# First block of a two-block transformer kernel: the 31-tap convolution as Toeplitz products on TensorE, rotary tiles of four heads, attention in pairs of heads

## What is computed

```
proj = rms_norm(h, g_mix_pre) @ w_in       # w_in 1024 x 1696: q_a 384 | kv_a 256 | k_rope 32 | conv 2 x 512
q  = rms_norm(q_a) @ w_q_b                 # 8 heads of 64 plain + 32 rotary columns
kv = rms_norm(kv_a) @ w_kv_b               # 8 heads of 64 key + 64 value columns
q_rope, k_rope = apply_rope(...)           # x1*cos - x2*sin, x1*sin + x2*cos
attn = causal softmax((q_nope.k_nope + q_rope.k_rope) * 96**-0.5) @ v
a, gate = split(conv)
c = causal_depthwise_conv(a * sigmoid(gate), conv_w, conv_b)   # 31 taps, 512 channels
c = silu(layer_norm(c, conv_ln_g, conv_ln_b))
mix = concat([attn, c]) @ w_o              # w_o 1024 x 1024
h = h + rms_norm(mix, g_mix_post)
```

## Time and profile before

| | us |
|---|---|
| median of 3 runs | 2088.38 |
| the profiled execution's own time | 2087.02 |
| its span (first to last instruction) | 2085.2 |
| TensorE busy | 1899.2 (91%) |
| VectorE busy | 1111.9 (53%) |
| ScalarE busy | 712.1 (34%) |
| GpSimd busy | 776.4 (37%) |
| mean granted TensorE clock | 0.944 |

### The profile page before, as it was taken

One profiled execution on the slowest core, in us unless ns is written; L12 is line 12 of the kernel. 1 busy time (PEld: TensorE's weight loads), 2 busy tenths in 40 slices (PEclk: granted clock), 3 DMA queues, 4 the chain that ended last, 5 costly groups with the idle time before them and its releaser, 6 DMA issues.

```text
span 2085.2 us, 24117 instructions
## 1 busy us (share of the span) xinstructions
PE 1899.2 (91%) x8716; PEld 1523.6 (73%) x8716; DVE 1111.9 (53%) x1734; ACT 712.1 (34%) x1162; POOL 776.4 (37%) x323
## 2 busy tenths in 40 slices
PE   7957775899999979999999999999978899999997
PEld 5735453788888757788888888898755578888885
DVE  6987837844344566333634443740488727333444
ACT  4234333322222234213322222332368833222221
POOL 3344031353444333434544454344300034444541
PEclk9977887999999989999999999997879999999998
DMA  5211011133233222495332323233111122333331
GB/s 174 67 54 41 11 61 41 61 104 98 85 112 95 85 72 85 91 195 139 122 93 88 101 92 110 81 101 101 46 26 31 52 64 86 106 98 91 91 94 57
DMA packets 52170, 177.34 MB, mean 85 GB/s; under 512 B 5528, under 2 KB 5912, under 8 KB 52089
## 3 DMA queue, kind: packets, MB, share of 16 engines
q1 hardware_dynamic: 47952, 166.22, 25.4%
q10 hardware_dynamic: 4136, 10.02, 3.4%
HBM read 166.75 MB, written 9.47 MB: 85 GB/s over the span
## 4 chain that ended last, share of the span: by engine, by line
PE 78%; DVE 16%; ACT 3%; issue 2%; DMA 0%; POOL 0%; DVEq 0%; ACTq 0%
PE ps L394 25%; PE ps L395 24%; PE ps L396 24%; DVE arena L1333 4%; DVE acc L1261 1%; DVE arena L1905 1%; DVE arena L1888 1%; PE ps L749 1%; PE ps L726 1%; DVE h L1517 1%; PE ps L714 1%; DVE rstd L1266 1%; DVE arena L1515 1%; DVE arena L1448 1%; PE ps L448 1%
## 5 line engine op out<-in xcount | busy, mean ns | idle before, releaser
L351 POOL TENSOR_TENSOR WL<-raw,WH 128x1024 fp32r<-128x1024 f32 x301 | 751.0, 2510 | 1257.9 <-ACT WH L788 1257.9
L394 PE MATMUL ps<-XH,WH 128*128 128x512 f32 (+1 forms) x1296 | 512.4, 395 | 61.4 <-DVE XL L1271 32.8
L395 PE MATMUL ps<-XL,WH 128*128 128x512 f32 (+1 forms) x1296 | 508.5, 392 | 0.0
L396 PE MATMUL ps<-XH,WL 128*128 128x512 f32 (+1 forms) x1296 | 508.0, 392 | 0.0
L788 ACT ACTIVATE WH<-raw 128x1024 fp32r<-128x1024 f32 x301 | 309.9, 1052 | 545.5 <-PE ps L396 492.7
L394 PE MATMUL ps<-HH,WH 128*128 128x512 f32 x1056 | 419.6, 397 | 35.7 <-DVE arena L1415 18.0
L396 PE MATMUL ps<-HH,WL 128*128 128x512 f32 x1056 | 415.5, 393 | 0.0
L395 PE MATMUL ps<-HL,WH 128*128 128x512 f32 x1056 | 415.5, 393 | 0.0
L394 PEld LDWEIGHTS ps<-XH,WH 128*128 128x128 f32 x1296 | 252.0, 194 | 121.9 <-issue 47.7
L396 PEld LDWEIGHTS ps<-XH,WL 128*128 128x128 f32 x1296 | 252.1, 195 | 49.5
L395 PEld LDWEIGHTS ps<-XL,WH 128*128 128x128 f32 x1296 | 252.2, 195 | 48.8 <-issue 0.7
(11 more groups left out here) (207 smaller groups left out, 1675.0 us busy)
## 6 DMA issues: line engine op xcount, KB each, us to landing
raw<-in_weights SPq DMA_DIRECT2D x301, 512.0 KB, 3.6
tab<-arena ACTq DMA_DIRECT2D x1, 5120.0 KB, 78.4
arena<-tab SPq DMA_DIRECT2D x16, 256.0 KB, 3.7
ftab<-arena ACTq DMA_DIRECT2D x1, 2080.0 KB, 23.7
h<-in_xT SPq DMA_DIRECT2D x8, 256.0 KB, 7.9
out_T<-h SPq DMA_DIRECT2D x8, 256.0 KB, 2.1
arena<-ftab ACTq DMA_DIRECT2D x4, 256.0 KB
arena<-in_pT ACTq DMA_DIRECT2D x1, 512.0 KB, 3.6
```

What stands on the lines that cost most here:

```text
L351: nc.gpsimd.tensor_tensor(WL[:, s, :], raw[:, s, :], WH[:, s, :].bitcast(f32), SUB)\
L394: nc.tensor.matmul(out, wh, xh, start=start, stop=False)
L395: nc.tensor.matmul(out, wh, xl, start=False, stop=False)
L396: return nc.tensor.matmul(out, wl, xh, start=False, stop=stop)
```

## The change

On TensorE: each of the 8 groups of 64 channels becomes 16 float32 matmuls of 128 rows, 128 outputs and 256 columns (`conv_group`). `U` holds even tokens of a group in partitions 0 to 63 and odd tokens in 64 to 127, with 15 columns of zeros ahead; `tz` holds, for one group, the diagonal blocks of the tap values. VectorE makes `tz` by one multiplication of 2048 elements a row (`lag_products`), two buffers deep, and ScalarE takes the results out of PSUM with the bias (`conv_out`). `CPE = 4` puts all four channel tiles there, so `convolve` has no steps left. In w_in the conv units come first (`SOURCE`), then q_a, k_rope, kv_a.

The rotary table fills 128 partitions, and the columns of w_q_b and of k_rope are regrouped while ScalarE and GpSimd split the weights (`pieces`, 3 instructions instead of one for each of two units of w_in, 6 for each pair of w_q_b units). Four heads' rotary rows come out of one tile. Attention runs in 4 pairs, as in the second block, with 32-row matmuls added for the rotary part; the maximum is no longer found and scaled in steps of its own. The layer norm of the convolution is spread over the attention loop, its sums over channels are made by four float32 matmuls each (`ln_total`), and w_o starts with the conv rows, between the transposes and products of the last pairs.

The diff, cut to its core:

```diff
+CPE = 4
+GPE, LAGS = 2 * CPE, 16
+        WOH = [XH[:, 6, :], XH[:, 7, :], HH[:, 2, :], HH[:, 3, :]] + [XH[:, c, :] for c in range(4)]
+        SOURCE = [0, 1, 2, 3, 8, 9, 12, 13, 4, 5, 6, 7, 10, 11] + list(range(14, 20)) + [...]
+        KEYS1, HEADS1 = (10, 11), (14, 16)
...
+            def conv_group(g):
+                if g >= 4:
+                    pe.wait_ge(sems["ce_done"], 2 * (g - 3))
+                pe.wait_ge(sems["tz_ok"], g + 1)
+                pe.wait_ge(*m["u_ok"].next(2))
+                for k in range(LAGS):
+                    at = 64 * (2 * LAGS - 2 - 2 * k)
+                    last = nc.tensor.matmul(ps[:, 4 + g % 4, 256 * (g // 4):256 * (g // 4) + 256], tz[:, g % 2, at:at + P],
+                                            U[:, g, LAGS - 1 - k:UW - k], start=k == 0, stop=k == LAGS - 1,
+                                            skip_group_check=True)
+                last.then_inc(sems["tz_used"], 1)
+            def ln_total(x, ready, done):
+                for c in range(4):
+                    ready(c)
+                    last = nc.tensor.matmul(ps[:, 6, :], ones[:, :], x[:, c, :], start=c == 0, stop=c == 3)
+                last.then_inc(sems[done], 1)
+            def mla_scores(n, step):
...
+                for qs in STEPS2[step]:
+                    w, at, q = P * (qs + 1), P * (qs == 1), slice(qs * P, (qs + 1) * P)
+                    for k, (low, of) in enumerate(((XH, HH), (XH, HL), (XL, HH))):
+                        for r in range(2):
+                            nc.tensor.matmul(ps[:, 2 * (c % 2) + r, at:at + w], low[HALF[r], n, q],
+                                             of[HALF[r], KN[n], 0:w], start=k == 0, stop=False)
+                    for k, (low, of) in enumerate(((XH, HH), (XH, HL), (XL, HH))):
+                        for r in range(2):
+                            i = 32 * (2 * (n % 2) + r)
+                            last = nc.tensor.matmul(ps[:, 2 * (c % 2) + r, at:at + w], low[i:i + 32, 4 + n // 2, q],
+                                                    of[i:i + 32, KRR, 0:w], start=False, stop=k == 2)
...
             project(2, 4, 2, XH, XL, m["x_lo"])
             total(7)
-            for _ in range(4):
+            for _ in range(6):
                 project(2, 4, 2, XH, XL)
             total(2)
-            for _ in range(2):
-                project(2, 4, 2, XH, XL)
+            conv_group(0)
             total(1)
+            for g in range(1, GPE):
+                if g == 3:
+                    pe.wait_ge(sems["norm_std"], m["norm_sum"].n)
+                conv_group(g)
...
+            ln_total(cacc, convolved, "ln_sum")
+            for n in range(NP1 + 2):
+                if n < NP1:
+                    if n % 2 == 0:
+                        pe.wait_ge(sems["q1_lo"], n // 2 + 1)
+                    mla_scores(n, 0)
+                    mla_scores(n, 1)
+                if n >= 2:
+                    mla_values(n - 2)
+                if n == 1:
+                    ln_total(lnsq, lambda c: pe.wait_ge(sems["ln_sq"], c + 1), "ln_var")
+                if n < NP1:
+                    mla_scores(n, 2)
+                if n == NP1:
+                    pe.wait_ge(sems["l1_done"], 8 * NP1)
+                    w_o((0, 1), m["cv_lo"])
+                if 1 <= n <= NP1:
+                    for r in range(2):
+                        mla_transposes(n - 1, r)
+                if n == NP1:
+                    w_o((1, 2), m["cv_lo"])
-            project(4, 2, 4, XH, XL, m["x_lo"], part=(0, 2))
-            total(3)
-            pe.wait_ge(*m["conv_xc"].next(4))
-            total(3)
-            project(4, 2, 4, XH, XL, m["x_lo"], part=(2, 4))
-            project(4, 2, 4, XH, XL)
+            w_o((2, 4), m["at_lo"])
+            project(4, 2, 4, WOH, WOL, cols=lambda x, c: x[c])
             total(7)
...
+            def conv_out(g):
+                act.wait_ge(sems["tz_used"], g + 1)
+                ch = 8 - GPE + g
+                for f in range(2):
+                    nc.scalar.activation(cacc[64 * (ch % 2):64 * (ch % 2) + 64, ch // 2, 1 - f::2],
+                                         ps[HALF[f], 4 + g % 4, 256 * (g // 4):256 * (g // 4) + 256], ACT.Identity,
+                                         bias=small[HALF[f], BIAS2 + g:BIAS2 + g + 1])\
+                      .then_inc(sems["ce_done"], 1)
...
+            def lag_products(g):
+                if g >= 2:
+                    dve.wait_ge(sems["tz_used"], g - 1)
+                V.tensor_tensor(tz[:, g % 2, :].rearrange("p (e n) -> p e n", n=64),
+                                stack.unsqueeze(1).to_broadcast([P, 2 * LAGS, 64]),
+                                taps_of[:, g, :].unsqueeze(2).to_broadcast([P, 2 * LAGS, 64]), MUL).then_inc(sems["tz_ok"], 1)
...
-            for n in range(H1 + 1):
-                if n < H1:
-                    logits(n, JOBS1[n])
-                if n >= 1:
-                    normalise(n - 1, JOBS1[n - 1])
-                convolve(8)
```

More of the change, by code:

```diff
@@ L481, in values @@
                 for g, kts in enumerate(VALUES):
-                    pe.wait_ge(*m["pt_act"].upto(3 * n + g + 1))
+                    if g == 0:
+                        pe.wait_ge(sems["p1_g0"], 2 * n + 2)
+                    else:
+                        pe.wait_ge(sems["p1_rest"], 4 * n + 2 + g)
                     for kt, at in kts:
-                        done = nc.tensor.matmul(job.out[:, kt * P:S], job.v(kt), job.pt(n)[:, at:at + S - kt * P],
-                                                start=first and kt == 0, stop=last and (g, kt) == (2, 2),
-                                                skip_group_check=True)
@@ L487, in values @@
-                done.then_inc(*m["o_done"].tick())
+                        for r in range(2):
+                            hd = 2 * n + r
+                            last = nc.tensor.matmul(ps[HALF[r], 6, kt * P:S], V1[:, kt, hd * VD:(hd + 1) * VD],
+                                                    PT1[r][:, at:at + S - kt * P], start=kt == 0, stop=(g, kt) == (2, 2),
+                                                    skip_group_check=True)
+                last.then_inc(sems["v1_done"], 1)
@@ L783, in upper @@
                 while b.ahead < min(upto, NU):
+                    if b.ahead in KEYS1 + HEADS1 and not b.du:
+                        u, n = b.ahead, 2 if b.ahead in HEADS1 else 1
+                        for k in range(u, u + n):
+                            act.wait_ge(raw_in[k % NSLOT], 16 * (k // NSLOT + 1))
+                        act.wait_ge(sems["used"], u + n - NSLOT)
+                        for out, src in pieces(u):
+                            last = nc.scalar.activation(out(WH), src, ACT.Copy)
+                        last.then_inc(sems["whi"], n)
+                        m["whi"].n += n
+                        b.ahead += n
+                        continue
                     u, s, i = b.ahead, b.ahead % NSLOT, b.du * b.state.i if b.du else 0
@@ L877, in _ @@
             upper(b.u + 4)
-            gates()
-            upper(b.u + 3)
             root(V1[:, 1, :], KVR)
```

577 lines of the change are left out of this document (302 added, 275 removed).

## The result

Median of the changed kernel: 2067.91 us (2066.39 to 2070.28, 4 runs), beside 2092.47 us (2087.84 to 2097.45, 4 runs) of the kernel before on the same chip. The ratio is 0.9883, 95% interval 0.9852 to 0.9915: faster by 1.2%, and the forecast was 2065. On a later chip the same two stood at 2068.02 and 2092.17, ratio 0.989 (0.9874 to 0.9905). The profiled execution took 2066.39 against 2087.02: 20.6 us less, where 22.3 were forecast. By the medians it is 24.6 us less: the profiled execution of the kernel before, at 2087.02, is shorter than each of the four runs in its median (2087.84 at least), so some of the 4 us between the two figures are scatter between executions.

A forecast was written before the change was run, and what follows sets the result against it. VectorE was taken to bound the stretch from 97 to 281 us, its taps 94.1 us. The terms put w_o's end at 293.3 instead of 315.6: 22.3 less than 2087.02, 2064.7, given as 2065, range 2046 to 2085.

The forecast's parts named there:

- Start: Before the first products: 36 small VectorE copies ahead of the first XL cost 1.1 us; w_in with its sum ends at 97.1.
- Convolution: First block's convolution on TensorE: 0.227 us a pass, 32 passes a group, 58 us for 8 groups, ending at 163.2.
- rival D: Convolution: weight loads not hidden, a pass costs 0.42 us instead of 0.227, +49, total 2114; chance 0.06.
- The wait for table 2: Before convolution group 2: TensorE waits 4.1 us for VectorE's tap table, ready at 116.6; 3 us more for low clock.
- w_q_b and w_kv_b: After the convolution: 27.2 us of matmuls plus 1.5 for bank handovers, end 191.9; with the channel sum 195.3.
- Attention: First block's four pairs with layer norm: first logits at 198.1, bare loop ends at 239.1, with additions 260.6.
- The 15.5 us: Attention: ScalarE's added layer norm work 11.1, a wait of about 2 for VectorE, output copies 2.4, all counted whole.
- the rotary term: Attention scores: added rotary matmuls cost TensorE 1 us in all, between 0 (all hidden) and 5 (none).
- The w_o term: End of attention: two w_o units of 10.9 us between last transposes and products cost 5, the middle of 0 to 10.9.
- B: Attention: TensorE gets through the first two pairs at 1.2 GHz, +11, total 2076; chance 0.18.
- C: Attention: not quicker, pairs take the old 80 us and layer norm's 11 on top, +25, total 2090; chance 0.07.
- A: Better: inverses done in time (no 4.1 wait, no 3 of low clock), w_o units wholly hidden (5), total 2053; chance 0.22.

The follow-up runs named there:

- Experiment 1: Changed kernel with VectorE's block of 36 small copies moved behind its first XL work; 2067.19 us.
- experiment 2: Changed kernel with VectorE making the tap table of convolution group 2 ahead of the second inverse instead of behind it; 2059.37 us against 2066.39.
- experiment 3: Changed kernel with ScalarE's output copies moved ahead of the Silu block; 2064.83 us.
- experiment 4: Changed kernel with the Silu block one pair later and w_o's first unit behind the last transposes; 2064.58 us.
- experiment 6: Changed kernel without the 32-row rotary products in the first block's scores; 2066.86 us.
- experiment 8: Changed kernel with the two w_o units of the attention loop's last step issued behind the loop; 2071.51 us.
- three tiles: Changed kernel with group 2's tap table made ahead of the second inverse and one of four convolution tiles on VectorE; 2055.86 us, ratio 0.9820 to the kernel before.
- table 2 early: Changed kernel with group 2's tap table made ahead of VectorE's second inverse; median 2061.35 us, ratio 0.9855 to the kernel before.

## Why the prediction was right, point by point

**Start: mis-sized.** I took 1.1 us. The first matmul comes 4.8 us later (15.27, before 10.48), and w_in with its sum ends at 99.5, not 97.1: 3.5 us late against before. VectorE's timeline, and GpSimd's of the same time:

```profile
7.20 0.18 DVE L1363 COPY arena<-vec 64x31 f32<-64x31 f32 x1
7.47 2.30 DVE L1363 COPY arena<-vec 64x31 f32<-64x31 f32 x1
...
11.52 2.20 DVE L1363 COPY arena<-vec 64x31 f32<-64x31 f32 x1
...
14.37 1.42 DVE L1343 SCALAR_TENSOR_TENSOR XL<-h,vec,XH 128x512 fp32r<-128x512 f32 x2
...
18.84 2.90 DVE L1343 SCALAR_TENSOR_TENSOR XL<-h,vec,XH 128x512 fp32r<-128x512 f32 x1
```

```profile
7.38 2.35 POOL L370 TENSOR_TENSOR WL<-raw,WH 128x1024 fp32r<-128x1024 f32 x1 [6.29 <-ACT WH L854]
11.33 2.35 POOL L370 TENSOR_TENSOR WL<-raw,WH 128x1024 fp32r<-128x1024 f32 x1 [1.61 <-ACT WH L854]
18.07 5.88 POOL L370 TENSOR_TENSOR WL<-raw,WH 128x1024 fp32r<-128x1024 f32 x2 [4.40 <-ACT WH L854]
```

A pair of copies takes 0.27 us, but two of them end only when GpSimd's subtraction beside them does (9.77 and 9.73, 13.72 and 13.68). They also start at 5.11, when the vector has landed, so that 9.3 us of copies ended at 14.4; the two long ones are 4.1 of it. The Trainium skill has a rule (GPSIMD Engine Reference, Specifications: the SBUF interfaces are shared with VectorE, with contention in a two-port mode or with two inputs). The trace agrees for steps with two inputs: the XL step at 18.84 takes 2.90 us beside two subtractions, where it takes 0.74 alone. The copies have one input, and whether they ran in such a mode the trace doesn't say; 2 of 36 were held.

Experiment 1 shows the copies' price, 1.8 us at the w_in mark, more than I had for the whole. The other 1.7 of the 3.5 can be read there too. The first matmul is 0.2 later than before. TensorE waits for 4.06 us in w_in instead of 2.91: 2.40 of it at 17.98, for an XL step of 2.84 us that ran beside a subtraction, and 0.60 at 64.10 for VectorE (L1434), which the changed kernel has at 65.93 and the kernel before has not. And it is busy for 83.0 us instead of 82.6, at a clock of 0.96 instead of 1.00.

**Convolution: right.** 0.227 a pass forecast; 107.30 - 99.53 less the sum of 0.86 is 6.91 for 32, 0.216 each. The loads lie beneath (rival D has fallen):

```profile
L466 PE MATMUL ps<-arena 128*128 128x256 f32 x256 | 58.6, 392 | 4.0 <-DVE arena L1374 4.0
L466 PEld LDWEIGHTS ps<-arena 128*128 128x128 f32 x256 | 50.3, 197 | 12.9 <-DVE arena L1374 4.4 <-issue 1.0
L1374 DVE TENSOR_TENSOR arena<-arena 128x2048 f32<-128x2048 f32 x6 | 13.7, 2288 | 20.5 <-PE ps L466 20.5
```

The wait for table 2 was forecast at 4.1 and is 4.01, in its place, with its releaser; it hides two small misses, since TensorE got there 1.7 us later (114.2, not 112.5) and the table was ready at 118.3, not 116.6. The 3 us of clock behind it are shown by experiment 2, as 2.9 here and 1.6 in others. The stretch ends near 163, as forecast: 2.4 us too late at its start, and 256 passes 2.8 us shorter.

**w_q_b and w_kv_b.** Forecast 195.3 for the end of the channel sum, 193.5 measured. No handover of banks made TensorE wait (busy for 31.00 of 31.00), where I had 1.5. The first logits come at 196.0, forecast 198.1.

**Attention.** Forecast to end at 260.6, it ended at 259.5; from the first logits it took 63.5 us, forecast 62.5. ScalarE was the engine without gaps in the place that I named, but its price stands in two waits of 5.35 and 2.52 us with a clock of 0.60 to 0.64 from 225 to 234. Its timeline:

```profile
223.56 1.28 ACT L1029 ACT_TABLE_LOAD   x1
224.85 2.93 ACT L1029 ACTIVATE arena<-arena,vec 128x512 f32<-128x512 f32 x4
227.69 1.14 ACT L1033 ACTIVATE XH<-arena 128x512 fp32r<-128x512 f32 x2
228.73 1.13 ACT L1033 ACTIVATE HH<-arena 128x512 fp32r<-128x512 f32 x2
229.77 0.58 ACT L1004 ACTIVATE arena<-ps 128x512 f32<-128x512 f32 x1
```

The 15.5 us that I added whole fit the sum, but no run took that work away, so their size is not shown; experiments 3 and 4 show only that moving it within ScalarE gains 1.3 us at best. By experiment 6 the rotary term of 1 is not above about 1 (a run without those products ended 1.4 later, give or take 2.2). The w_o term was mis-sized: by experiment 8 it is 10.9 - 3.7 = 7.2 rather than 5, with the scatter between 5 and 9.4. Of the rivals, B had the clock low over the first two pairs, where it was 1.00 up to 220 us (what B describes did happen in the profiled run of three tiles, 0.83 over 180 to 200 us); C had the pairs no quicker; A was right that table 2's wait and its clock cost 7 us, and wrong that they would not arise; its other half, w_o's two units hidden wholly, experiment 8 rules out.

**The sum.** At the last matmul of w_o 23.3 us were gained, where 22.3 were forecast; at the end 20.6. What was lost behind it: the norm's sum at 295.53 took 2.07 us instead of 1.23, and the next matmul is ahead by 22.4. Between the norm at 709.47 (731.50 before) and the transposes at 1494.57 (1513.00 before) the lead falls from 22.0 to 18.4, with the same work. All of that goes in the first third. From 723.84 to 775.50 (745.86 to 796.02 before) 1.5 us are lost, 1.1 of them in waits for VectorE (5.9 us instead of 4.8). Up to 847.65 (867.67 before) 0.5 are lost, with a clock of 0.98 instead of 1.00. The next window loses 1.6, and the one behind it nothing. After:

```profile
847.65:971.65 124.00, 124.00 (x531) 101.00 (x532) 44.52 (x58) 35.10 (x42) 53.24 (x22) 0.97 0.74 153
971.65:1320.72 349.07, 349.07 (x1539) 288.76 (x1538) 165.88 (x180) 94.56 (x113) 165.09 (x64) 1.00 0.33 98
```

and before, the same work:

```profile
867.67:990.07 122.40, 122.40 (x532) 100.44 (x532) 42.32 (x58) 35.21 (x42) 52.52 (x22) 0.99 0.76 155
990.07:1339.13 349.06, 349.06 (x1539) 288.66 (x1538) 165.85 (x180) 94.53 (x113) 165.08 (x64) 1.00 0.32 98
```

From 1320.72 (1339.13) to the transposes the lead stays at 18.4. 2.2 us come back by the end. The loss is no cost of the change: the stretch takes 781.5 us before and 785.1 in both profiles of the changed kernel, but 782.4 to 782.5 in experiments 1, 3, 4 and 6, whose code there is the same, and 785.1 and 787.9 in the two profiles of table 2 early. Why the clock and these waits differ between executions stays open.

The recorded sum has a slip: 2064.7 and the 1.4 us to the median are 2066.1, not 2065. And that it lands within 1 us at w_o is in part luck, since misses cancel: the start 2.4 too late, the convolution 2.7 shorter, w_q_b to the first logits 1.8 shorter, attention 1.0 longer. What is shown is the mechanism: the convolution's length on TensorE, the wait for table 2 with its clock, and VectorE no longer the bound.

## What to carry to other kernels

Moving a stretch from a full engine to another pays until the other is full: with the whole convolution on TensorE, VectorE was busy for 28.7 of 66 us, and three tiles of four there were faster than four. A wait of TensorE can be worth more than its length, 4.0 us of wait and 1.6 to 3 of clock here, so the operand that it waits for goes first in its producer's order, ahead of long work with no reader yet. Where another engine sets the pace, as ScalarE in attention, extra products cost less than can be told from the scatter, and moving that engine's work about gains little. Before a single run is read, two executions of one kernel should be laid side by side: here they differ by 2.2 us within the first 290 us, with all waits of attention equal.

## What the runs showed of the hardware that was not expected

Two copies of 64 x 31 elements took 2.30 and 2.20 us instead of 0.18, each until a GpSimd subtraction of 128 x 1024 beside it ended. Full-size VectorE steps were held as well: XL steps of 128 x 512 took 2.84 and 2.90 us instead of 0.74. Later, eight VectorE products of 64 x 256 took 6.47 us in all beside six GpSimd subtractions of 128 x 512 (6.25 in all); of the 16 such products of the kernel half take 0.43 or less, the longest 2.65.

Work taken away from TensorE in a stretch where it waits can save nothing: without the rotary products (96 instructions) it waited 14.9 us in attention instead of 8.6, at a clock of 0.81, 0.74 and 0.91 in three windows of 20 us where it had 1.00, 0.83 and 1.00, and the end was 1.4 us later. A lower clock there is not tied to the edit alone: two executions of one kernel had 0.84 and 0.74 over 220 to 240 us.
